# Feed-forward gate and up columns computed by seven block products of half width, two columns at a time

## The reference, cut to what matters

```
h2 = rms_norm(x, norm_ffn[l])
x = x + (jax.nn.silu(h2 @ w_ffn_gate[l]) * (h2 @ w_ffn_up[l])) @ w_ffn_down[l]
...
def swiglu(h, w1, w3, w2):
    return (jax.nn.silu(h @ w1) * (h @ w3)) @ w2
...
for l in range(DEPTH_2):
    x = x + 0.5 * swiglu(rmsnorm(x, ffn1_norm[l]), ffn1_w1[l], ffn1_w3[l], ffn1_w2[l])
    # a mixer on rmsnorm(x), then attention to a memory, each added to x
    x = x + 0.5 * swiglu(rmsnorm(x, ffn2_norm[l]), ffn2_w1[l], ffn2_w3[l], ffn2_w2[l])
return rmsnorm(x, final_norm)
```

## Time and profile before

| | |
|---|---|
| runs | 3230.31 us median of 3 (3230.3 to 3232.1) |
| span of the profiled execution | 3228.2 us |
| instructions | 39623 |
| PE busy | 3208.3 us (99%), 14786 matmuls |
| weight loads (PEld) busy | 2632.0 us (82%) |
| DVE busy | 1695.3 us (53%), 2482 instructions |
| ACT busy | 1164.5 us (36%), 1847 instructions |
| DMA | 313.32 MB, 97 GB/s |

### The profile page before, as it was taken

One profiled execution on the slowest core, in us unless ns is written; L12 is line 12 of the kernel. 1 busy time (PEld: TensorE's weight loads), 2 busy tenths in 40 slices (PEclk: granted clock), 3 DMA queues, 4 the chain that ended last, 5 costly groups with the idle time before them and its releaser, 6 DMA issues.

```text
span 3228.2 us, 39623 instructions
## 1 busy us (share of the span) xinstructions
PE 3208.3 (99%) x14786; PEld 2632.0 (82%) x14786; DVE 1695.3 (53%) x2482; ACT 1164.5 (36%) x1847; POOL 0.2 (0%) x4
## 2 busy tenths in 40 slices
PE   9999999999999999999999999999999999999999
PEld 7777778788888888888887888888888888788887
DVE  6564455564544545346755554344543676465443
ACT  5673555532222222233533322222222344332222
POOL 0000000000000000000000000000000000000000
PEclk9999999999999999999999999999999999999999
DMA  4333333232222222232322222222223233132222
GB/s 146 102 95 98 97 100 105 85 117 93 97 98 98 96 94 96 98 114 79 118 85 66 94 95 97 98 98 94 95 98 103 97 98 111 46 105 97 93 96 92
DMA packets 90696, 313.32 MB, mean 97 GB/s; under 512 B 10192, under 2 KB 12624, under 8 KB 90192
## 3 DMA queue, kind: packets, MB, share of 16 engines
q1 hardware_dynamic: 83376, 294.69, 27.5%
q10 hardware_dynamic: 7200, 16.97, 1.7%
HBM read 309.52 MB, written 2.10 MB: 97 GB/s over the span
## 4 chain that ended last, share of the span: by engine, by line
PE 95%; DVE 2%; ACT 2%; issue 1%; DMA 0%; SPq 0%; ACTq 0%; DVEq 0%
PE ps L1101 29%; PE ps L1103 29%; PE ps L1102 29%; PE ps L1300 1%; PE ps L1386 1%; PE ps L1289 1%; PE ps L1177 1%; PE ps L1399 0%; PE ps L1423 0%; PE ps L1334 0%; PE ps L1281 0%; PE ps L1338 0%; PE ps L1278 0%; PE ps L1317 0%; PE ps L1328 0%
## 5 line engine op out<-in xcount | busy, mean ns | idle before, releaser
L1101 PE MATMUL ps<-x_hi,whi 128*128 128x512 f32 x2400 | 945.0, 394 | 0.0
L1103 PE MATMUL ps<-x_hi,wlo 128*128 128x512 f32 x2400 | 934.6, 389 | 0.0
L1102 PE MATMUL ps<-x_lo,whi 128*128 128x512 f32 x2400 | 934.0, 389 | 0.0
L1440 ACT ACTIVATE whi<-raw 128x1024 fp32r<-128x1024 f32 (+1 forms) x555 | 583.1, 1053 | 895.3 <-DMA raw<-in_weights 893.2
L1727 DVE TENSOR_TENSOR wlo<-raw,whi 128x1024 fp32r<-128x1024 f32 x553 | 675.3, 1223 | 418.5 <-ACT whi L1440 409.7
L1101 PEld LDWEIGHTS ps<-x_hi,whi 128*128 128x128 f32 x2400 | 450.7, 188 | 97.2 <-issue 3.9
L1103 PEld LDWEIGHTS ps<-x_hi,wlo 128*128 128x128 f32 x2400 | 450.5, 188 | 94.6
L1102 PEld LDWEIGHTS ps<-x_lo,whi 128*128 128x128 f32 x2400 | 450.8, 188 | 94.2 <-issue 2.4
L1101 PE MATMUL ps<-h_hi,whi 128*128 128x512 f32 (+1 forms) x902 | 346.4, 384 | 0.0
L1103 PE MATMUL ps<-h_hi,wlo 128*128 128x512 f32 (+1 forms) x902 | 346.2, 384 | 0.0
L1102 PE MATMUL ps<-h_lo,whi 128*128 128x512 f32 (+1 forms) x902 | 346.2, 384 | 0.0
(11 more groups left out here) (295 smaller groups left out, 3303.7 us busy)
## 6 DMA issues: line engine op xcount, KB each, us to landing
raw<-in_weights SPq DMA_DIRECT2D x553, 512.0 KB, 3.3
bias<-in_biasB ACTq DMA_DIRECT2D x16, 384.0 KB, 3.2
bias<-in_biasA ACTq DMA_DIRECT2D x16, 256.0 KB, 3.2
mem_raw<-in_mem ACTq DMA_DIRECT2D x3, 1024.0 KB, 7.0
x_res<-in_x SPq DMA_DIRECT2D x8, 256.0 KB, 6.6
x_res<-in_x ACTq DMA_DIRECT2D x8, 256.0 KB, 3.2
out_x<-x_res SPq DMA_DIRECT2D x16, 128.0 KB, 1.8
raw<-in_weights SPq DMA_DIRECT2D x2, 256.0 KB, 4.0
```

What stands on the lines that cost most here:

```text
L1101: pe.matmul(out, hi, xhi, start=start, stop=False)
L1102: pe.matmul(out, hi, xlo, start=False, stop=False)
L1103: return pe.matmul(out, lo, xhi, start=False, stop=stop)
L1440: return act.activation(out, in_, ACT.Copy, scale=scale)
```

## The change

Gate and up columns are taken in pairs of f: two gate and two up columns of 128, all eight chunks deep. Seen as a product of a 2x2 block matrix of weights (which f of the pair, which half of the eight chunks) with a 2x2 block matrix of activations (which half of the chunks, which half of the 512 tokens), each pair is computed by Strassen's seven block products in Winograd's form, P1 to P7. Each product has eight tiles (four chunks, for gate and for up), three matmuls a tile, on 256 tokens. Pair 0 (f = 0 and 1) stays as it was (`plain`), the pairs 1 to 10 take the new way.

- Weights of a pair come as four blocks A11, A12, A21, A22 (a `wload` of 512 KB each on SP, the same bytes as the four units before). DVE forms S1 = A21 + A22, S3 = A11 - A21, S2 = S1 - A11, S4 = A12 - S2 (`wsum`). Each of the seven forms used is rounded on ACT (`whigh`) and its low part subtracted on DVE (`wlow`).
- Activations need four sums T1 to T4 of scaled halves, once a stage (`xt`, `thigh` on ACT; `tform`, `tlow` on DVE), in four parts p, of which three stand beside the columns m = 4 to 6 that make the residual (`toward_ffn`) and the fourth behind the first plain unit.
- P1, P6, P7, P4 accumulate one over the other in one PSUM bank (bank 0 or 3, by pairs in turn), P5 and P3 share bank 1, P2 has bank 2. ACT copies the bank's state out (`kept`) after P1, P5 and P6, before the next product may write there. DVE adds the pieces to the four result blocks (`block`), scales them (`rmul`), and rows go on to SiLU (now in place), product and split. The high part's rounding (`fhigh`) is on ACT now.
- P4 of a pair runs behind P1 and P5 of the next pair.
- `h_hi`, `h_lo` hold six rows instead of 22, so down columns follow every two pairs: 4 rows of all eight columns, four times, then the last six rows (for m < 4 as four rows and two rows). Each pass has an eviction of its own.
- The loops over f are written out, and so is the loop of weight loads.

```diff
--- before.py
+++ after.py
+FORM_OF = {"P1": "A11", "P2": "A12", "P3": "S4", "P4": "A22", "P5": "S1", "P6": "S2", "P7": "S3"}
+PRODUCT_OF = {form: name for name, form in FORM_OF.items()}
+MOVING = {"P5": 0, "P6": 1, "P7": 2, "P4": 3}
...
+    def toward_ffn(m, n, gain, j):
+        if m == 3:
+            for i, form in [(1, form) for form in SET] + [(2, "A21"), (2, "A22")]:
+                step("wload", n=n, i=i, form=form, free=("evac", j))
+        if m >= 4:
+            if m < DC - 1:
+                moving_sums(n, m - 4, gain)
+            if 5 <= m < DC - 1:
+                step("tlow", n=n, p=m - 5)
+    def moving_sums(n, p, gain):
+        step("xt", n=n, p=p, gain=gain)
+        step("tform", n=n, p=p)
+        step("thigh", n=n, p=p)
...
+        s.open_units(u0 + AHEAD - 1)
+        step("ffn", n=n)
+        step("plain", n=n, unit=u0, c=0)
+        step("fsum", n=n)
+        s.open_units(u0 + 2)
+        moving_sums(n, 3, gain)
+        step("tlow", n=n, p=2)
+        total(1, "S1")
+        high(1, "S1", "A11")
+        total(1, "S3", "S2")
+        low(1, "A11")
+        high(1, "S2")
+        step("froot", n=n)
+        step("fscale", n=n, unit=u0, c=0)
+        row("silu", 0)
+        step("plain", n=n, unit=u0 + 1, c=1)
+        s.open_units(u0 + 3)
+        step("tlow", n=n, p=3)
+        low(1, "S1")
+        step("fscale", n=n, unit=u0 + 1, c=1)
+        row("fmul", 0)
+        row("fhigh", 0)
+        step("plain", n=n, unit=u0 + 2, c=2)
+        total(1, "S4")
+        low(1, "S2")
+        row("flow", 0)
+        high(1, "A12")
+        low(1, "A12")
+        step("fscale", n=n, unit=u0 + 2, c=2)
+        row("silu", 1)
+        step("plain", n=n, unit=u0 + 3, c=3)
+        step("fscale", n=n, unit=u0 + 3, c=3)
+        row("fmul", 1)
+        row("fhigh", 1)
+        high(1, "S4", "S3")
+        row("flow", 1)
+        low(1, "S4", "S3")
+        def odd_pair(i):
+            y, o = i + 1, i - 1
+            product(i, "P1")
+            load(y, "A11", (i, "P1"))
+            kept(i, "P1")
+            s.open_units(u0 + 4 + 4 * (i // 2) + 3)
+            product(i, "P5")
+            kept(i, "P5")
+            if o:
+                product(o, "P4")
+                load(y, "A22", (o, "P4"))
+                block(o, "C21")
+                row("silu", 2 * o + 1)
+            high(y, "A11")
+            if o:
+                row("fmul", 2 * o + 1)
+                row("fhigh", 2 * o + 1)
+            if o:
+                row("flow", 2 * o + 1)
+            high(i, "A22")
+            low(i, "A22")
+            total(y, "S1")
+            high(y, "S1")
+            product(i, "P6")
+            kept(i, "P6")
+            total(y, "S3", "S2")
+            low(y, "A11")
+            high(y, "S2")
+            product(i, "P2")
+            load(y, "A12", (i, "P2"))
+            block(i, "C11")
+            low(y, "S1")
+            product(i, "P3")
+            block(i, "C12")
+            step("rmul", n=n, i=i, row=0)
+            row("silu", 2 * i)
+            total(y, "S4")
+            high(y, "S4")
+            row("fmul", 2 * i)
+            row("fhigh", 2 * i)
+            product(i, "P7")
+            load(i + 2, "A21", (i, "P7"))
+            block(i, "C22")
+            row("flow", 2 * i)
+            step("rmul", n=n, i=i, row=1)
+            low(y, "S2")
+            high(y, "S3", "A12")
...
+        def even_pair(i):
...
+            low(i, "S3")
+            product(i, "P5")
+            kept(i, "P5")
+            product(o, "P4")
+            load(q, "A22", (o, "P4"))
+            block(o, "C21")
+            row("silu", 2 * o + 1)
+            low(i, "A12")
+            row("fmul", 2 * o + 1)
+            row("fhigh", 2 * o + 1)
+            low(i, "S4")
+            row("flow", 2 * o + 1)
+            high(i, "A22")
+            low(i, "A22")
+            if more:
...
+        odd_pair(9)
+        even_pair(10)
+        fs, t1 = range(16, NF), (u0 + 20) * UT
+        for m in range(4):
+            if m == 2:
+                product(10, "P4")
+                block(10, "C21")
+                row("silu", NF - 1)
+                row("fmul", NF - 1)
+                row("fhigh", NF - 1)
+                row("flow", NF - 1)
+            down(t1 + 4 * m, fs[0:4], m, fs[0:4] if m == 0 else ())
+        step("ffn_end", n=n)
         for m in range(DC - last):
-            j = s.job(t1 + m * NF, NF, rhs="h", n=T, evac="back" if back else "resid", m=m, c=c, first=(m == 0), norm=n)
+            late = m < 4
+            j = down(t1 + (16 + 2 * m if late else 6 * m), fs[4:] if late else fs, m, fs[4:] if m == 0 else (),
+                     "back" if back else "resid")
             step("refresh", n=n + 1, m=m, gain=gain_next, need=("x", m) if back else ("evac", j))
+            if back or gain_next.startswith("ffn1"):
+                toward_ffn(m, n + 1, gain_next, j)
...
+                elif kind == "prod":
+                    n, i, name = a["n"], a["i"], a["name"]
+                    form = FORM_OF[name]
+                    low = FORM_LOW[place_of(i, form)]
+                    pe.wait_ge(*on("form_ready", (n, i, form)))
+                    if i == 1 and name in MOVING:
+                        pe.wait_ge(*on("tl", (n, 3)))
+                    if name == "P1":
+                        out = chain_bank(i)
+                        pe.wait_ge(*on(*(("block", (n, i - 2, "C21")) if i > 2 else ("fg" if i == 1 else "fu", (n, i - 1)))))
+                    elif name == "P5":
+                        out = PS[:, 1, :]
+                        pe.wait_ge(*on(*(("block", (n, i - 1, "C12")) if i > 1 else ("fu", (n, 0)))))
+                    elif name == "P2":
+                        out = PS[:, 2, :]
+                        pe.wait_ge(*on(*(("block", (n, i - 1, "C11")) if i > 1 else ("fg", (n, 1)))))
+                    elif name == "P3":
+                        out = PS[:, 1, :]
+                        pe.wait_ge(*on("kept", (n, i, "P5")))
+                    else:
+                        out = chain_bank(i)
+                        pe.wait_ge(*on(*{"P6": ("kept", (n, i, "P1")), "P7": ("kept", (n, i, "P6")),
+                                         "P4": ("block", (n, i, "C22"))}[name]))
+                    opens = name in ("P1", "P2", "P5")
+                    for at in range(UT):
+                        w, k = divmod(at, 4)
...
+                        to = out[:, w * HALF:(w + 1) * HALF]
+                        hi, lo = high_tile(form, at), low[:, at * P:(at + 1) * P]
+                        pe.matmul(to, hi, xhi, start=opens and at == 0, stop=False, skip_group_check=True)
+                        pe.matmul(to, hi, xlo, start=False, stop=False, skip_group_check=True)
+                        mm = pe.matmul(to, lo, xhi, start=False, stop=at == UT - 1, skip_group_check=True)
+                    mm.then_inc(*sig("prod", (n, i, name)))
...
+                elif kind == "kept":
+                    n, i, name = a["n"], a["i"], a["name"]
+                    act.wait_ge(*on("prod", (n, i, name)))
+                    if i > 1:
+                        act.wait_ge(*on("block", (n, i - 1, {"P1": "C11", "P5": "C22", "P6": "C12"}[name])))
+                    copy(kept_in(name), PS[:, 1, :] if name == "P5" else chain_bank(i)).then_inc(*sig("kept", (n, i, name)))
...
+                elif kind == "tform":
+                    n, p = a["n"], a["p"]
+                    dve.wait_ge(*on("xt", (n, p)))
+                    b11, b12, b21, b22 = XT[:, 0, 0:HALF], XT[:, 0, HALF:T], XT[:, 1, 0:HALF], XT[:, 1, HALF:T]
+                    t1, t2, t3, t4 = (TF[:, p, k, :] for k in range(4))
+                    dve.tensor_tensor(t1, b12, b11, ALU.subtract).then_inc(*sig("tf", (n, p, 1)))
+                    dve.tensor_tensor(t3, b22, b12, ALU.subtract).then_inc(*sig("tf", (n, p, 3)))
+                    dve.wait_ge(*on("tf", (n, p, 1)))
+                    dve.tensor_tensor(t2, b22, t1, ALU.subtract).then_inc(*sig("tf", (n, p, 2)))
+                    dve.wait_ge(*on("tf", (n, p, 2)))
+                    dve.tensor_tensor(t4, b21, t2, ALU.subtract).then_inc(*sig("tf", (n, p)))
...
+                elif kind == "block":
+                    n, i, name = a["n"], a["i"], a["name"]
+                    of, kept, by, to = {"C11": (PS[:, 2, :], "P1", "P2", 0), "C12": (PS[:, 1, :], "P6", "P3", 1),
+                                        "C22": (chain_bank(i), "P5", "P7", 2), "C21": (chain_bank(i), None, "P4", 1)}[name]
+                    to = CB[:, to, :, :]
+                    dve.wait_ge(*on("prod", (n, i, by)))
+                    dve.wait_ge(*on("fhl", (n, {"C11": 2 * i - 2, "C12": 2 * i - 1, "C22": 2 * i - 1, "C21": 2 * i}[name])))
+                    if kept:
+                        dve.wait_ge(*on("kept", (n, i, kept)))
+                        dve.tensor_tensor(to, in_halves(of), in_halves(kept_in(kept)), ALU.add).then_inc(*sig("block", (n, i, name)))
+                    else:
```

(4 more changed lines are left out.)

423 lines of the change are left out of this document (299 added, 124 removed).

## The result

The changed kernel takes 3252.9 us (median of 4 runs, 3252.5 to 3254.7) against 3231.1 us before (4 runs). The ratio is 1.0069, with a 95% interval from 1.0055 to 1.0083. The forecast was 3251 us. The profiled execution has a span of 3250.8 us, 22.6 us more than before.

The account below looks back on a forecast made before the run. PE was taken as the bound, busy for 3208 of 3228 us. Span 3228.2 - 81 (products) + 0 (steady pairs) + 100 (entries) + 2 (end) = 3249 us, with 2 us around it 3251 us; range 3200 to 3285 us.

Parts of the forecast that it names:

- The products: Feed-forward matmuls on PE: a pair takes 20.14 us instead of 21.77, so 50 pairs save 81 us.
- The steady pairs: In the steady stretch of pairs, PE waits 0 us for DVE and ACT; bounds 0 and 30 us.
- The entries: At the five feed-forward stage entries, uncovered PE waits add 100 us together; bounds 25 and 125 us.
- (a): At stage entries, the sums beside m = 4 to 6 make PE wait for x_lo, 53 us over five stages.
- (b): Fourth plain column of each entry: PE waits 5.6 us for the unit's low part, 28 us over five stages.
- (c): First new pair of each entry: P6 waits 2.0 us and P7 1.8 for ACT's copies, 19 us in all.
- The clock rival: Behind ten entry waits without cover, PE returns at half clock: 27 us lost, 3278 us; chance 0.08.
- the kernel's end: Last column in halves, with DVE's final operations ahead of its eviction: end 2 us later, between 0 and 4.
- The faster rival: At the entries, DVE and ACT overlap more, waits fall to about half, 50 us: 3201 us; chance 0.22.

## Why the prediction came out right, step by step

**The products, -81.** Right. The narrow matmul goes at 0.12 us beside a DVE that is busy for 80%, as it did in the earlier trace rows beside one nearly idle: 20.16 us a pair, where 20.14 was forecast.

**The steady pairs, 0.** Right: no wait. The tightest margins of 0.2 us held. DVE's share is 80%, forecast was 77. What P4's place covers, though, is far more than I gave it. The loss without it is 310 us, not some 80 as I expected before that run.

**The entries, +100.** Measured from PE's starts (from the last columns before the first plain one to the end of the first new pair, less the same work at full rate): 14.5, 27.6, 16.0, 21.4 and 16.0 us, 95.5 in all. The forecast's stages were 16.0, 28.9, 16.0, 23.0 and 16.0. By the forecast's three terms:

| term | forecast, us | measured, us |
|---|---|---|
| (a) round beside m = 4 to 6 | 8.2 | 8.0 |
| (a) wait for x_lo, from whole columns | 6.6 each | 5.5 each |
| (a) from the down columns of a stage; with the copy back | 13.6; 19.5 | 11.2; 15.3 |
| (b) wait for the fourth unit | 5.6 each | 2.0 to 3.5 |
| (c) P6 and P7 | 2.0 + 1.8 each | 1.5 + 1.3 in three stages, 0 + 0.5 and 0 + 1.3 in two |

The lay-out by hand of the in-order queues was right to 0.2 us a round. Each wait then came out shorter than forecast. In part this is the clock: in the first stage PE runs at half speed for 6.8 us between the wait for x_lo and that for the fourth unit, and so arrives there some 3 us later. The chain (b) is as long as forecast, 20.5 us from the eviction of m = 7 at 703.8 to the start of PE's fourth column at 724.3, where 20.9 was said. PE spent a part of it slow instead of idle. That is why waits of 66 us in the table make 95.5 us of loss, and why keeping the clock up brought nothing. So the terms were too dear as waits, by a third in all, and right as the length of the chain. Why the waits from down columns came out 2.4 and 4.2 us shorter than laid out isn't shown.

**The clock rival** had the event right (half clock behind waits of this length) and nearly its size: ten columns of 5.4 us are 54 us at half rate, and 61 were measured. It put most of the cost on the next wait, and all of it went there. The 1 us a stage that it kept for the clock doesn't stand in the forecast's sum of 100 us, and no run shows that it should.

**Small things missed.** The mixers' first group behind the second and fourth stage now waits 1.6 us each for x_lo, which I had at nothing. With the stages' ends (0.4 us each) and the kernel's end (+2.4, forecast +2) these make 8 us. So -81 + 95.5 + 8 = +22.5, where the spans differ by 22.6. The forecast of 3251 us owes part of its closeness to entries 4.5 us too dear and extras 6 us too cheap.

**The faster rival** named the right lever with the wrong agent: it asked for more overlap by itself, and the order rules that out. With all the orders changed the same kinds of waits fall from 71 to 39 us, and the kernel to 3209.6, near the 3201 that it gave.

## What to carry to other kernels

When work is added beside a loop on two engines that serve each other, lay out one round of both queues and look for an operation of one that needs nothing of the other but stands behind one that does. Here two such moves together, a rounding whose data were already in memory and a subtraction put where its engine waited, were worth 36 of the 95 us, and turned a loss into a gain, while spreading the same work over more rounds brought nothing. Price a product that is moved away from its consumer by what is queued on the consumer's engine at that place, not by the handshake. A clock drop behind a wait costs its full price only if the next wait doesn't absorb it.
